# Keys of the memory: each product over 128 rows issued as two over 64 rows, into two banks

## The reference

```python
def memory_cross_attention(h, mem_n, wq, wkv, wo):
    B, S, _ = h.shape
    M = mem_n.shape[1]                       # 256 memory tokens
    q = (h @ wq).reshape(B, S, XATTN_HEADS, XATTN_HEAD_DIM)
    kv = (mem_n @ wkv).reshape(B, M, 2, XATTN_HEADS, XATTN_HEAD_DIM)
    k, v = kv[:, :, 0], kv[:, :, 1]          # k: 256 tokens x 1024 features
    s = jnp.einsum('bqhd,bkhd->bhqk', q, k).astype(jnp.float32) * (XATTN_HEAD_DIM ** -0.5)
    p = jax.nn.softmax(s, axis=-1).astype(v.dtype)
    ...
# per layer: mem_n = rmsnorm(mem, mem_norm[layer])
```

## Time and profile before

| | |
|---|---|
| runs | 1441.24, 1441.82, 1441.78 us; median 1441.78 |
| profiled execution | 1441.34 us, span of its instructions 1439.6 us |
| PE | busy 1427.9 us (99%), 6782 matmul records |
| PEld | busy 1186.3 us (82%) |
| DVE, ACT, POOL | 731.7 us (51%), 524.8 us (36%), 103.4 us (7%) |
| granted clock of TensorE | 0.998 of full speed over the span |
| DMA | 147.50 MB, mean 102 GB/s |

### The profile page before, as it was taken

The page is one execution under the profiler, slowest core; times in us unless marked ns, Lnnn a source line. Parts: engine busy times, 40 slices in busy tenths (PEclk is TensorE's granted clock), DMA queues, the critical chain, the costliest instruction groups (busy, mean ns, idle before and its releaser), DMA issues.

```text
span 1439.6 us, 17918 instructions
## 1 busy us (share of the span) xinstructions
PE 1427.9 (99%) x6782; PEld 1186.3 (82%) x6782; DVE 731.7 (51%) x1032; ACT 524.8 (36%) x789; POOL 103.4 (7%) x90
## 2 busy tenths in 40 slices
PE   8999999999999999999999999999999999999998
PEld 8888888888888888888877778988888888888887
DVE  6656555454444443334568765755544444443332
ACT  5632544333323323222645614544433323322221
POOL 0012200200000000000201101100020000000010
PEclk9999999999999999999999999999999999999999
DMA  9731321232332333333321212542132332323221
GB/s 326 253 98 59 114 76 45 88 103 88 102 99 90 102 103 103 102 103 124 103 74 59 80 53 73 176 147 73 45 117 88 102 100 89 102 91 108 98 83 59
DMA packets 41513, 147.50 MB, mean 102 GB/s; under 512 B 4848, under 2 KB 4976, under 8 KB 41456
## 3 DMA queue, kind: packets, MB, share of 16 engines
q1 hardware_dynamic: 37728, 136.59, 28.4%
q10 hardware_dynamic: 3728, 10.10, 2.1%
HBM read 144.57 MB, written 2.10 MB: 102 GB/s over the span
## 4 chain that ended last, share of the span: by engine, by line
PE 95%; DVE 2%; ACT 1%; DMA 1%; issue 1%; POOL 0%; ACTq 0%; POOLq 0%
PE acc L1392 28%; PE acc L1393 27%; PE acc L1394 27%; PE acc L1440 3%; PE acc L1442 3%; PE acc L1441 3%; PE aux L1736 1%; PE acc L1760 1%; PE aux L1748 1%; DMA memT<-in_mem_t 1%; PE aux L1394 0%; PE aux L1393 0%; PE aux L1392 0%; DVE xpt_lo L1117 0%; DVE xp L1134 0%
## 5 line engine op out<-in xcount | busy, mean ns | idle before, releaser
L855 DVE TENSOR_TENSOR w_lo<-raw,w_hi 128x1024 fp32r<-128x1024 f32 x255 | 314.7, 1235 | 327.7 <-ACT w_hi L442 327.4
L1392 PE MATMUL acc<-u_hi,w_hi 128*128 128x512 f32 x1056 | 413.1, 391 | 0.0
L1394 PE MATMUL acc<-u_hi,w_lo 128*128 128x512 f32 x1056 | 411.1, 389 | 0.0
L1393 PE MATMUL acc<-u_lo,w_hi 128*128 128x512 f32 x1056 | 411.0, 389 | 0.0
L442 ACT ACTIVATE w_hi<-raw 128x1024 fp32r<-128x1024 f32 x255 | 267.9, 1052 | 376.9 <-DVE tmp L1209 192.1
L1392 PEld LDWEIGHTS acc<-u_hi,w_hi 128*128 128x128 f32 x1056 | 198.3, 188 | 43.0 <-issue 2.4
L1394 PEld LDWEIGHTS acc<-u_hi,w_lo 128*128 128x128 f32 x1056 | 198.3, 188 | 41.1
L1393 PEld LDWEIGHTS acc<-u_lo,w_hi 128*128 128x128 f32 x1056 | 198.4, 188 | 40.4
L1392 PE MATMUL acc<-act_hi,w_hi 128*128 128x512 f32 (+1 forms) x374 | 141.6, 379 | 0.0
L1394 PE MATMUL acc<-act_hi,w_lo 128*128 128x512 f32 (+1 forms) x374 | 140.9, 377 | 0.0
L1393 PE MATMUL acc<-act_lo,w_hi 128*128 128x512 f32 (+1 forms) x374 | 140.8, 377 | 0.0
(11 more groups left out here) (185 smaller groups left out, 1596.6 us busy)
## 6 DMA issues: line engine op xcount, KB each, us to landing
raw<-in_weights SPq DMA_DIRECT2D x255, 512.0 KB, 3.5
hT<-in_x_t ACTq DMA_DIRECT2D x4, 512.0 KB, 6.5
x_tok<-in_x ACTq DMA_DIRECT2D x4, 512.0 KB, 7.1
out_h<-y_tok SPq DMA_DIRECT2D x4, 512.0 KB, 2.9
mem_tok<-in_mem ACTq DMA_DIRECT2D x1, 1024.0 KB, 12.6
memT<-in_mem_t ACTq DMA_DIRECT2D x3, 256.0 KB, 6.6
decay<-in_decay ACTq DMA_DIRECT2D x1, 768.0 KB, 4.7
raw<-in_weights SPq DMA_DIRECT2D x2, 256.0 KB, 4.8
```

Source lines behind the costliest of these rows:

```text
L855: dve.tensor_tensor(w_lo[:, s, :], raw[:, s, :], w_hi[:, s, :].bitcast(F32), ALU.subtract)\
L1392: pe.matmul(out, w_h, x_h, start=first, stop=False)
L1393: pe.matmul(out, w_h, x_l, start=False, stop=False)
L1394: return pe.matmul(out, w_l, x_h, start=False, stop=last)
```

## The change

Each of the 24 products of a K unit is made as two: one over partitions 0 to 63 of weights and memory, one over partitions 64 to 127. They are issued one after the other, the first into the bank `acc[t % 4]`, the second into a bank of `aux`, so that each bank holds half of the sum over input features. ACT copies the aux half into `xk`, DVE adds the acc half and then multiplies by `rstd_mrow`. The plan of `aux` gets 16 entries ("half", layer, j), each freed by ACT. Nothing else is changed; values of the memory, queries and all later stages are as they were.

```diff
@@ aux_plan
+    for j in range(3):
+        add(("half", 0, j), "a")
     add("mem row", "v")
+    for j in range(3, KT):
+        add(("half", 0, j), "a")
     add(("row", 0), "v")
...
-        add(("mean", 3 * layer + 1), "v")
-        add(("row", 3 * layer + 1), "v")
+        if layer:
+            for j in range(KT):
+                add(("half", 1, j), "a")
+                if j == 2:
+                    add(("mean", 4), "v")
+                if j == 5:
+                    add(("row", 4), "v")
+        else:
+            add(("mean", 1), "v")
+            add(("row", 1), "v")
@@ scalar
+            def k_half_copy(layer, j):
+
+                t = aux_at["half", layer, j]
+                act.wait_ge(aux_done, t + 1)
+                act.activation(xk[:, j, :], auxs[t % 4][:, 0:M], ACT.Copy).then_inc(aux_free_a, 1)
...
                 if j < 4:
                     act.dma_start(hT[:, 2 * j:2 * j + 2, :], d["x_t"][:, 2 * j:2 * j + 2, :]).then_inc(x_in[j], 16)
+                k_half_copy(0, j)
...
                 split(KV_UNIT[1] + n + LEAD)
+                if n < KT:
+                    k_half_copy(1, n)
                 kv_hi_parts(1, n)
@@ vector, kv_drain
                 if j < KT:
-                    ins = dve.tensor_tensor(kv_tile(j, xk, xv), acc(t)[:, 0:M], rstd_mrow[:, :], ALU.mult)
+                    dve.wait_ge(aux_free_a, freed_a(aux_at["half", layer, j]))
+                    n = step(dve.tensor_tensor(xk[:, j, :], xk[:, j, :], acc(t)[:, 0:M], ALU.add))
+                    dve.wait_ge(dve_step, n)
+                    ins = dve.tensor_tensor(xk[:, j, :], xk[:, j, :], rstd_mrow[:, :], ALU.mult)
@@ tensor
+            def k_unit(layer, j, before=None):
+
+                n, t, b = KV_UNIT[layer] + j, KV_ACC[layer] + A_K + j, aux_at["half", layer, j]
...
+                acc_free(t)
+                aux_free(pe, b)
+                outs = (accs[t % 4][:, 0:M], auxs[b % 4][:, 0:M])
+                for k in range(KT):
...
+                    for q, (wt, mt) in enumerate(((w_hi, mem_hi), (w_hi, mem_lo), (w_lo, mem_hi))):
+                        for e in range(2):
+                            rows = slice(e * (P // 2), (e + 1) * (P // 2))
+                            ins = pe.matmul(outs[e], wt[rows, s, w], mt[rows, k, :], start=(k == 0 and q == 0),
+                                            stop=(k == KT - 1 and q == 2))
+                            if k == KT - 1 and q == 2:
+                                ins.then_inc(aux_done if e else acc_done, 1)
```

More of the change, by code:

```diff
@@ L1422, in rows_unit @@
                 ins.then_inc(acc_done if last else unit_used, 1)
+            def k_unit(layer, j, before=None):
+                n, t, b = KV_UNIT[layer] + j, KV_ACC[layer] + A_K + j, aux_at["half", layer, j]
+                s = n % RING
+                if n == 0:
+                    pe.wait_ge(first_lo, 1)
+                else:
+                    weights_in(n)
+                acc_free(t)
+                aux_free(pe, b)
+                outs = (accs[t % 4][:, 0:M], auxs[b % 4][:, 0:M])
+                for k in range(KT):
+                    if n == 0 and k == KT // 2:
+                        weights_in(0)
+                    if before is not None:
+                        before(k)
+                    w = slice(k * P, (k + 1) * P)
+                    for q, (wt, mt) in enumerate(((w_hi, mem_hi), (w_hi, mem_lo), (w_lo, mem_hi))):
[5 more added lines that the diff above has]
+                                ins.then_inc(aux_done if e else acc_done, 1)
             def cols_units(n0, t0, x_h, x_l, tiles, before=None, after=None):
@@ L1486, in kv_proj @@
                 for j in range(KT):
-                    rows_unit(u0 + j, a0 + A_K + j, mem_hi, mem_lo,
-                              before=(lambda k: pe.wait_ge(mlo_ready, 8 * layer + k + 1)) if j == 0 else None)
+                    k_unit(layer, j, before=(lambda k: pe.wait_ge(mlo_ready, 8 * layer + k + 1)) if j == 0 else None)
                     if after is not None:
@@ L1500, in _ @@
             for j in range(KT):
-                rows_unit(u0 + j, a0 + A_K + j, mem_hi, mem_lo,
-                          before=(lambda k: pe.wait_ge(mlo_ready, k + 1)) if j == 0 else None)
+                k_unit(0, j, before=(lambda k: pe.wait_ge(mlo_ready, k + 1)) if j == 0 else None)
                 if j == 2:
```

## The result

| | before | after |
|---|---|---|
| runs, median | 1441.24 us (18 runs, 1440.74 to 1441.82) | 1443.45 us (18 runs, 1443.02 to 1444.05) |
| ratio, 95% interval | | 1.0015, 1.0008 to 1.0021 |
| profiled execution, its span | 1441.34 us, 1439.6 us | 1443.08 us, 1441.2 us |
| granted clock over the span | 0.998 | 0.998 |

Halves cost 2.2 us (1.2 to 3.0 by the interval). That is within the 0.2% which the prediction had called hard to tell from no change. The two profiled spans differ by 1.6 us.

A forecast was written before the change was run, and what follows sets the result against it. The prediction took PE, busy 99% of the span, to bound the kernel. Pairs 0, edges 0.8 and layer 0's start 0.75 gave +1.5 us on 1441.8, so 1443.3 us; range 1438.5 to 1452, from the bounds of its own case 1441.8 to 1445.2.

The forecast's parts named there:

- The main term: K stages of both layers: a pair of half products costs what one whole product did, 120 ns, so 0 us.
- the 13 ns that stay: K stage matmuls: a float32r matmul costs its columns at 2.4 GHz plus 13 ns; halves were taken to keep this gap.
- The start of layer 0: PE's unit 4 in layer 0 waits for the drain of tile 0 and starts 0.75 us later, at about 23.8.
- the dependent pair: Drain of tile 0 on DVE, layer 0: an add and a dependent multiply take 0.45 us more.
- ACT's copies: Layer 0: two aux-half copies on ACT ahead of unit 5's rounding delay DVE's w_lo by 0.3 us.
- The edges: Nine switches between whole and half array, three in layer 0, six in layer 1, 0.09 us each: 0.8 us.
- The cover on DVE and ACT: K stage after the start: DVE's step of 2.25 us stays under PE's 2.88, so PE does not wait.
- The gap does not hide: Denies the faster rival: in every pair one half hides the other's 13 ns, 4.0 us back, 1439.3 us; chance 0.20.
- The halves do not run one after the other: Denies the slower rival: every pair pays its second matmul, 35 to 48.3 us more, 1479 to 1492 us; chance 0.17.

The follow-up runs named there:

- e8_halves128: Changed kernel with blocks 1 to 7 of each K unit moving only 128 of 256 tokens, row halves taking turns; 1458.95 us (one run).
- e7_whole128: Kernel before the change, whole array, with blocks 1 to 7 of each K unit moving only 128 of 256 tokens; 1455.73 us (one run).
- e5_early: Changed kernel with layer 0 tile 0's aux copy on ACT and its add on DVE moved earlier, leaving only the multiply; 1443.04 us, ratio 1.001.
- e6_layer0: Changed kernel with halves in layer 0 only, layer 1's K units as before the change; 1442.31 us, ratio 1.0008.
- e3_edges: Changed kernel with blocks 0, 2, 4, 6 of each unit on the whole array, the others in halves, 128 edges; 1488.72 us, ratio 1.0329.
- e1_grouped: Changed kernel with each block's three lower-half products issued first, then its three upper-half ones; 1443.36 us, ratio 1.0014.
- e2_apart: Changed kernel with all 24 lower-half products of a unit issued first, then all 24 upper-half ones; 1530.55 us, ratio 1.0619.
- e11_onehalf: Kernel before the change with K products over rows 0 to 63 alone, the upper half's left out; 1472.12 us (one run).

## Why the prediction was right

*The main term, 0 us for 384 pairs: right.* Partners start together and pairs come 120 ns apart, in layer 1 and, at full clock, in layer 0. The nearest rows had been column halves, and row halves do as they do. The reason given for the 13 ns that stay, that each half has the whole array's stream and load, fits e8_halves128: halving the rows shortens neither. One reading beside it was not sound. The prediction took 0.109 us for a load from ten transposes of 128 columns; but these are float32 passes, which by its own reading take two cycles per column, so their stream alone is 107 ns and the row says nothing of the load. e7_whole128 gives 0.111, so the value was right by luck.

*The start of layer 0, 0.75 us: right in kind, 0.52 in size.* Of its two parts the dependent pair was as said, 0.45 us. The other, 0.3 us for ACT's copies, was 0.11: I had put two copies ahead of unit 5's rounding as if DVE waited for all of it, but DVE had its own w_lo to do meanwhile. e5_early shows that the pair is a cause, and that it can't be had back fully; e6_layer0's trace shows that not every execution has the wait.

*The edges, 9 x 0.09 = 0.8 us: the term that was mis-sized.* Only seven of nine show: the two around `mem row` lie ahead of unit 4, which waits for DVE anyway. But an edge is not only the stop ahead of the first matmul. The second one is late as well, by 0.10 us, and this I had left out, because the earlier trace rows show the first matmul of a series and not its second. In the trace the seven are worth 0.22 + 1.02 = 1.24 us. e3_edges puts 0.19 us on one edge where both sides are dense streams; around `mean` two cost only 0.29, since the product behind the small matmuls had started its successor late before as well (0.20 us).

The two errors in the sum go opposite ways, 0.2 us too much at the start of layer 0 and 0.4 too little for the edges: 1.5 us were forecast, the trace shows 1.6 to 1.8, and that they are so near is in part luck. That 1443.3 us lie 0.15 from the measured 1443.45 is luck as well: the forecast stood on 1441.8, the median of three runs, and over 18 runs the kernel before takes 1441.24, from which the same sum gives 1442.7. The timed 2.2 us have an interval of 1.2 to 3.0, so the difference to the trace is not told apart from none. e6_layer0 gives +0.9 us for layer 0; the changed kernel's 0.74 and layer 1's 1.02 in the trace are in that proportion, as far as intervals of this width can say.

*The cover on DVE and ACT: right.* In the K stage of layer 1 PE waited for nothing; over 902 to 928 us DVE has 1.6 us more work, where 3.4 had been allowed for, and ACT 1.0, where 2.7 had been.

*The rivals.* The gap does not hide: 120 ns, not 109. The halves do not run one after the other as the change issues them. But the reason I had against it, that each pair is issued alternately, is not what protects them: e1_grouped has no alternation within three products and loses nothing. That rival came true with 24 matmuls of one half in a row (between three and 24 nothing was tried), and then with about twice the price that I gave it, since the clock falls too (e2_apart: +89 us, where the rival gave 35 to 48).

*What stays open.* Why a float32r matmul of 256 or 512 columns keeps 13 ns between streams. Whether column halves or quarters of rows would change that was not tried. What sets the clock is open in part. An idle row half made it fall in layer 1 (e2_apart, e11_onehalf). Frequent edges (e3_edges) and short matmuls (e7_whole128, e8_halves128) only kept it low at the program's start; in layer 1 they ran at 1.00. Why these matmuls ran at the full clock in layer 1 and did not reach it in layer 0 is not shown.

## What to carry to other kernels

Splitting a product that fills all 128 rows into row halves buys nothing: the halves run side by side and each keeps the full column count and the full weight load. It costs what surrounds it: 0.19 us at each change between whole and half array in a dense stream, and a second bank to add where the vector engines have no reserve. If row halves are used, keep them together in time, change halves at least every three matmuls (the most that was seen to cost nothing), and keep both at work, or the clock may fall with PE 100% busy.

## What the runs showed of the hardware

- Matmuls of one row half start ahead of up to three of the other half that stand before them in the program; within a half the order holds (e1_grouped, e2_apart).
- A change between whole and half array costs 0.09 us ahead of the first matmul and 0.10 ahead of the second, both ways (e3_edges).
- With 128 columns a float32r matmul starts every 112 ns, whether whole or as a pair of halves: the stream is not what bounds it, since one start comes after 0.06 us, and the weight load is what is left (e7_whole128, e8_halves128, `mean`).
- The granted clock fell to 0.50 in a stretch with PE busy all of the time, while one row half at a time was at work (e2_apart, e11_onehalf). At the program's start it stayed at the lower level for the whole K stage of 42 to 74 us in these two and in e3_edges, e7_whole128 and e8_halves128, by the distance of starts.
